# Attention of a two-layer hybrid block rebuilt: high and low values packed in one stationary tile, linear units inside the attention stages, first turns of a pair ahead of the next pair's scores

## What is computed

```python
def _gqa(q, k, v):
    s = jnp.einsum('bqkgd,bskd->bkgqs', q, k).astype(jnp.float32) * (HEAD_DIM ** -0.5)
    p = jax.nn.softmax(s, axis=-1).astype(v.dtype)
    return jnp.einsum('bkgqs,bskd->bqkgd', p, v)
...
        s = jnp.concatenate([s_nb.reshape(B, H, GRID_W, kr * kcn), s_ctx], axis=-1)
        p = jax.nn.softmax(s, axis=-1).astype(v.dtype)
...
def _merge(gz, oa, ob, oc, w_branch, w_out):
    ga, gb, gf = jnp.split(jax.nn.sigmoid(gz), N_BRANCH, axis=-1)
    y = ga * (oa @ w_branch[0]) + gb * (ob @ w_branch[1]) + gf * (oc @ w_branch[2])
    return y @ w_out
```

## Time and profile before

| | us |
|---|---|
| median of 3 runs (2630.68 to 2631.56) | 2631.35 |
| the profiled execution | 2630.05 |
| its span, first to last instruction | 2628.2 |
| TensorE busy | 2413.8 (92%) |
| VectorE busy | 1177.5 (45%) |
| ScalarE busy | 797.8 (30%) |
| GpSimd busy | 789.3 (30%) |
| mean granted clock of TensorE | 0.971 |

### The profile page before, as it was taken

One profiled execution on the slowest core, in us unless ns is written; L12 is line 12 of the kernel. 1 busy time (PEld: TensorE's weight loads), 2 busy tenths in 40 slices (PEclk: granted clock), 3 DMA queues, 4 the chain that ended last, 5 costly groups with the idle time before them and its releaser, 6 DMA issues. The chain is left out here.

```text
span 2628.2 us, 37990 instructions
## 1 busy us (share of the span) xinstructions
PE 2413.8 (92%) x13562; PEld 2184.1 (83%) x13562; DVE 1177.5 (45%) x2129; ACT 797.8 (30%) x1305; POOL 789.3 (30%) x368
## 2 busy tenths in 40 slices
PE   7989899998899949999999959999998996999996
PEld 2889889987799949999999948789887875788885
DVE  3784464132643175575572271646204543423234
ACT  4122353213532252211111142345224524322222
POOL 1322201332013232232232333320432044444444
PEclk9999999999999979999999979999999998999998
DMA  6621100141112332343342323110321134233333
GB/s 238 212 98 61 36 0 25 64 145 54 40 30 61 112 120 95 108 151 112 110 160 64 120 96 93 56 49 0 101 85 57 39 91 141 73 95 97 97 97 132
DMA packets 63019, 237.62 MB, mean 90 GB/s; under 512 B 7252, under 2 KB 7508, under 8 KB 61272
## 3 DMA queue, kind: packets, MB, share of 16 engines
q1 hardware_dynamic: 51552, 194.02, 22.8%
q10 hardware_dynamic: 11384, 42.48, 4.5%
HBM read 225.97 MB, written 10.49 MB: 90 GB/s over the span
## 5 line engine op out<-in xcount | busy, mean ns | idle before, releaser
L418 POOL TENSOR_TENSOR w_lo<-raw,w_hi 128x1024 fp32r<-128x1024 f32 x268 | 663.2, 2475 | 1460.1 <-ACT w_hi L525 1460.1
L525 ACT ACTIVATE w_hi<-raw 128x1024 fp32r<-128x1024 f32 x268 | 284.0, 1060 | 776.3 <-PE ps L1318 373.4
L1316 PE MATMUL ps<-h_hi,w_lo 128*128 128x384 f32 (+1 forms) x1152 | 419.3, 364 | 10.2 <-POOL h_lo L437 8.7
L1316 PE MATMUL ps<-h_hi,w_hi 128*128 128x384 f32 (+1 forms) x1152 | 416.6, 362 | 0.0
L1316 PE MATMUL ps<-h_lo,w_hi 128*128 128x384 f32 (+1 forms) x1152 | 416.6, 362 | 0.0
L1316 PEld LDWEIGHTS ps<-h_hi,w_lo 128*128 128x128 f32 x1152 | 216.3, 188 | 38.7 <-POOL h_lo L437 12.1
L1316 PEld LDWEIGHTS ps<-h_hi,w_hi 128*128 128x128 f32 x1152 | 216.2, 188 | 22.5
L1316 PEld LDWEIGHTS ps<-h_lo,w_hi 128*128 128x128 f32 x1152 | 216.3, 188 | 22.0
L1318 PE MATMUL ps<-h_hi,w_hi 128*128 128x384 f32 x576 | 192.4, 334 | 0.0
L1318 PE MATMUL ps<-h_lo,w_hi 128*128 128x384 f32 x576 | 192.4, 334 | 0.0
L1318 PE MATMUL ps<-h_hi,w_lo 128*128 128x384 f32 x576 | 192.4, 334 | 0.0
(11 more groups left out here) (175 smaller groups left out, 4522.6 us busy)
## 6 DMA issues: line engine op xcount, KB each, us to landing
raw<-in_stream SPq DMA_DIRECT2D x268, 512.0 KB, 3.6
ada_raw_gate_up<-in_w_ada SPq DMA_DIRECT2D x48, 512.0 KB, 6.0
ada_raw_fourier_in<-in_w_ada SPq DMA_DIRECT2D x24, 512.0 KB, 4.3
bias_sb<-in_bias ACTq DMA_DIRECT2D x16, 640.0 KB, 3.9
first_raw<-in_w_first SPq DMA_DIRECT2D x8, 1152.0 KB, 5.1
scratch<-xr ACTq DMA_DIRECT2D x16, 512.0 KB, 3.1
xr<-scratch ACTq DMA_DIRECT2D x14, 512.0 KB, 6.2
xr<-in_x_in ACTq DMA_DIRECT2D x8, 512.0 KB, 6.1
```

The source lines that it names most:

```text
L418: nc.gpsimd.tensor_tensor(w_lo[:, s, :], raw[:, s, :], w_hi[:, s, :].bitcast(F32), ALU.subtract).then_inc(S("lo_made"), 1)
L525: nc.scalar.activation(w_hi[:, s, :], raw[:, s, :], ACT.Copy).then_inc(S("hi_made"), 1)
L1316: last = nc.tensor.matmul(bank(0), tile, x[:, k, 0:split], start=start, stop=stop)
```

## The change

**Stages.** The gates of A (8 units) are computed inside attention A, and the later queries and keys of B (6 units) and the first two gates of B inside attention B. These are the fills: `fill` takes the 24 (or 48) steps of a unit and spreads them over the slots of a head. The merges of A and B shrink to 4 and 10 units, and `values`, with the first key unit, the first query unit and four value units, replaces `tokens_b`. Queries and keys of B come out of `columns` feature by feature, so they need no staging and no transposes; A's are transposed for two heads at once straight from `tok_a`. `stage` is gone from GpSimd.

**Attention.** The unit of work is a pair of query tiles, `ORDER` = (0,1), (3,2), (4,5); layer 1 has the first two. I call the handling of pair n a slot. Before the turns GpSimd multiplies `p_sb` with the reciprocal row sum (`normalise`). Turned blocks are split, `pt_hi` by ScalarE (`turned_hi`) and `pt_lo` by VectorE (`turned_lo`), in groups of at most 512 columns. The values are packed as [high | low] in one stationary tile of 128 columns, and each key tile takes two fp32r matmuls of up to 256 columns, one by `pt_lo` and one by `pt_hi`. The 128 output rows hold the high and the low share, which `move_half` (ScalarE) and `fold` (VectorE) add. `out_hi` (ScalarE) and `o_rest` (GpSimd) split the sum for the merge.

**Order.** In TensorE's program the first two groups of turns of pair n stand ahead of the scores of n+1. The attention loops are written out in full on all engines. The bias of B comes in two halves per head, the rope table is loaded in `tokens_a`, and several tiles have other places in SBUF.

```diff
+ORDER = ((0, 1), (3, 2), (4, 5))
...
-        add("merge", layer, t, 12, part=2)
-        add("attention", layer, t, part=0)
-        add("merge", layer, t, 12, part=0)
-        add("tokens_b", layer, t, 12)
-        add("attention", layer, t, part=1)
-        add("merge", layer, t, 12, part=1)
+        add("merge_c", layer, t, 12)
+        add("attention", layer, t, FILLS, part=0)
+        add("merge_a", layer, t, 4)
+        add("values", layer, t, 6)
+        add("attention", layer, t, FILLS, part=1)
+        add("merge_b", layer, t, 10)
...
+                def normalise(n, i):
+                    j, c = n % pairs, 2 * (n % 2) + i
+                    keys = P * len(key_tiles(branch, ORDER[j][i], i))
+                    pool.wait_ge(S("inverse"), at(ph, "inverse") + 2 * n + i + 1)
+                    p = p_sb[branch][n % 2][i][:, 0:keys]
+                    nc.gpsimd.tensor_tensor(p, p, row_inv[:, c:c + 1].broadcast_to([P, keys]), ALU.mult
+                                            ).then_inc(S("p_ready"), 1)
...
+                for n in range(HEADS * pairs):
+                    if n + 1 < HEADS * pairs:
+                        normalise(n + 1, 0)
+                    if n and (n - 1) // pairs % 2:
+                        o_rest(n - 1)
+                    if n + 1 < HEADS * pairs:
+                        normalise(n + 1, 1)
+                    f = fill_ended(ph, n - 1)
+                    if f is not None:
+                        lo_part(ph.unit + f + 2)
...
+                for n in range(count):
+                    groups = range(len(turn_groups(branch, n % pairs)))
+                    f = fill_ended(ph, n - 1)
+                    if n:
+                        move_half(n - 1)
+                    if f is not None:
+                        fill_out(f)
+                    turned_hi(n, 0)
+                    if n + 1 < count:
+                        probs(n + 1, 0)
+                    for g in groups[1:2]:
+                        turned_hi(n, g)
+                    if fill_halves(ph) == 2 and (n + 1) % pairs == 0 and n + 1 < count:
+                        gate_half((n + 1) // pairs, 0)
+                    if n and (n - 1) // pairs % 2:
+                        out_hi(n - 1)
+                    if n + 1 < count:
+                        probs(n + 1, 1)
+                    for g in groups[2:]:
+                        turned_hi(n, g)
+                    for name in slot_pieces(ph, n):
+                        piece(*name)
+                    if f is not None:
+                        act.wait_ge(S("unit_done"), ph.unit + f + 1)
+                        split(ph.unit + f + 2, f % 2)
+                        if branch == 1 and f < 6 and f % 2:
+                            key_copies(f // 2 + 1, at(ph, "fill_out") + f + 1)
+                    h, j = divmod(n, pairs)
+                    if branch == 1 and j < 2 and h + 1 < HEADS:
+                        load_bias(ph, h + 1, j)
+                move_half(count - 1)
+                out_hi(count - 1)
...
+                def turned_lo(n, g):
+                    order = turns["p", n, g]
+                    a, w = 512 * g, turn_width(branch, n % pairs, g)
+                    dve.wait_ge(S("hi_out"), at(ph, "hi_out") + order + 1)
+                    nc.vector.tensor_tensor(pt_lo[branch][:, a:a + w], ps[:, TURN_BANK[branch] + order % 2, 0:w], pt_hi[branch][:, a:a + w].bitcast(F32),
+                                            ALU.subtract).then_inc(S("lo_out"), 1)
...
+                def fold(n):
+                    h, j = divmod(n, pairs)
+                    a, rows = 2 * P * (n % 2), slice(HD * (h % 2), HD * (h % 2) + HD)
+                    dve.wait_ge(S("moved"), at(ph, "moved") + n + 1)
+                    if h > 1 and h % 2 == 0:
+                        dve.wait_ge(S("o_lo"), at(ph, "o_lo") + pairs * (h // 2 - 1) + j + 1)
+                    nc.vector.tensor_tensor(o_sum[branch][rows, j, :], ps[rows, OUT_BANK[branch], a:a + 2 * P], o_half[branch][rows, n % 2, :], ALU.add
+                                            ).then_inc(S("folded"), 1)
...
+                for n in range(count):
+                    groups = range(len(turn_groups(branch, n % pairs)))
+                    f = fill_ended(ph, n - 1)
+                    if n:
+                        fold(n - 1)
+                    if branch == 1 and f is not None and f < 6:
+                        filled = at(ph, "fill_out") + f + 1
+                        if f % 2:
+                            key_rest(f // 2 + 1, filled)
+                        else:
+                            query_rest(ph, f // 2 + 1, filled)
+                    if n + 1 < count:
+                        maximum(n + 1, 0)
+                        maximum(n + 1, 1)
+                    turned_lo(n, 0)
+                    if n + 1 < count:
+                        invert(n + 1, 0)
+                    for g in groups[1:2]:
+                        turned_lo(n, g)
+                    if n + 1 < count:
+                        invert(n + 1, 1)
+                    for g in groups[2:]:
+                        turned_lo(n, g)
+                    for name in slot_pieces(ph, n):
+                        piece(*name)
+                fold(count - 1)
...
+                                user = ORDER[j][0 if kt in key_tiles(branch, ORDER[j][0], 0) else 1]
+                                out_col, w = out_col + P * (user % 2), P
+                            a = 512 * g + 2 * P * x
+                            for pt in (pt_lo, pt_hi):
+                                last = nc.tensor.matmul(ps[:, OUT_BANK[branch], out_col:out_col + w], v, pt[branch][:, a:a + w],
+                                                        start=g == 0 and x == 0 and pt is pt_lo,
+                                                        stop=g == len(groups) - 1 and x == len(groups[g]) - 1 and pt is pt_hi,
+                                                        skip_group_check=True)
+                    if len(groups) - 1 in some:
+                        last.then_inc(S("attended"), 1)
...
+                for n in range(count):
+                    groups = range(len(turn_groups(branch, n % pairs)))
+                    for g in groups[:2]:
+                        turn(n, g)
+                    if n + 1 < count:
+                        score(n + 1, 0)
+                        score(n + 1, 1)
+                    fill(n, 0)
+                    for g in groups[2:]:
+                        turn(n, g)
+                    for name in slot_pieces(ph, n):
+                        piece(*name)
+                    attend(n, groups[:2])
+                    fill(n, 1)
+                    attend(n, groups[2:])
```

1116 lines of the change are left out of this document (633 added, 483 removed).

## The result

The changed kernel takes 2605.34 us (median of 4; 2595.60 to 2606.16), against 2631.01 for the kernel before in the same comparison: a ratio of 0.9894, with an interval of 0.9870 to 0.9917. Four more executions in a later comparison gave 2603.26 and 0.9898 (0.9882 to 0.9915). The forecast was 2605. It was right in size, but not every term behind it was, and one of the agreements is partly luck.

The account below looks back on a forecast made before the run. It saw TensorE's work and its pauses in the four attention stages as the bound. 635.8+13+9.6+7+398.4+17 = 1080.8 us against 1107.0, 26 less, gave 2605 us; forecast's own range 2570 to 2635, widened to 2565 and 2650.

Parts of the forecast that it names:

- The slot of A: Attention A: one query-tile pair with 768 keys takes 8.0 us, 8.7 where ScalarE also copies an output or gate.
- the 2% that I had added: Four attention stages: 13 us added, since the same walk gave 92.3 us for an old stage that takes 94.1.
- Normalising: GpSimd in attention: 1.42 us for 768 keys, priced by the add with a broadcast operand, 1.89 per 1024.
- the slow rival: GpSimd's in-place product takes 2.03 us for 768 keys and ends last; stages 43 us more, 2648 us; chance 0.15.
- The danger: VectorE held up while GpSimd works: said to be small here, as o_lo, which reads PSUM, stays under 0.70 us.
- The slot of B: Attention B: full slot 7.3 us, with the fill's bank emptied 8.4 or 9.0 to 9.4; 22.2 and 16.9 per head.
- the starts: Starts of the attention stages: 2.0 us twice for A, 2.8 us twice for B.
- the wait for the bias: Attention B of layer 1: half loads of the bias, taken as 3.2 us each, cost 7 us in all.
- 635.8 + 13 + 9.6 + 7: Four attention stages: walked lengths 635.8 us, plus the 2%, the stage starts and the bias wait.
- 398.4 + 17: Touched stages outside attention: 398.4 us, plus 17 for the fold ahead of merge B, values start and y_lo wait.
- The clock: Rival: with TensorE busy for some 76% of attention the granted clock could fall, 2635 to 2665 us; chance 0.05.
- 73 + 32: TensorE work saved: 73 us in probabilities times values, 32 us in transposes.

Follow-up runs that it names:

- Scores first: Changed kernel, but TensorE computes the scores of pair n+1 before the first two turns of pair n: 2548.01 us, ratio to before 0.9694.
- normalising: Changed kernel with GpSimd normalising only 16 of each tile's 256 to 768 keys, work left out: 2575.30 us, the four attention stages 19.0 us less.
- two thirds: Changed kernel with two thirds of each fill, in place of one half, ahead of the last turn: 2585.42 us.
- without half of the fills: Changed kernel with every second of the first 23 matmul steps of each half unit inside attention not issued: 2604.18 us.
- overlapped emptying: In branch B VectorE takes the first head's low part once ScalarE has copied that half: 2586.24 us on the changed kernel, 2536.31 with scores computed first.

## Why the prediction came true, step by step

**The slot of A.** Forecast 8.0 us for a full slot, 8.7 with a copied output or gate between the exponentials, 6.5 and 7.2 to 7.8 around the context pair. Measured 7.93, 8.60, 5.97 to 6.45, and 7.7 to 8.4. The walked lengths of the two stages, 188.0 and 140.6, were measured as 189.0 and 141.2 without the 2% that I had added. Scores first (forecast 50 less in the stages, measured 50.3), normalising (20, measured 19) and two thirds (A of layer 0: 183.7, measured 183.5) use the same terms, so the mechanism is shown and not only the sum.

**Normalising.** Forecast 1.42 us for 768 keys from the add with a broadcast operand in the earlier trace rows, measured 1.47. The in-place product of two full tiles, which the slow rival was built on, is not its like. In the earlier trace rows I read 0.96 to 2.68 us as the stretching of one instruction; they are two shapes, 128x768 at 0.96 in layer 0 and 128x512 at 2.68 in layer 1, where GpSimd works beside it. The danger is thus larger than I wrote for two tiles in SBUF, and the forecast does not rest on it: the new low parts, which read PSUM, took 0.68.

**The slot of B was mis-sized.** I had 22.2 us per head in layer 0; two heads in a row took 24.0 and 23.7 (blocks of scores begin at 590.95, 614.93 and 638.64), 3.3 more. One part is the emptying of the fill's bank, for which I had a slot of 8.4. The copies take 1.62 together and the low parts 1.92, TensorE's pause is 2.8 us, and at the key units, where a stretch at the lower clock follows, the slot lasts 9.6; at the query units it lasts 8.1 to 8.4. That is 0.9 of the 3.3. The larger part lies in the other slots. In every second head GpSimd also makes the low part of the output, 0.73 us between its two normalisings, and ScalarE the high one between the exponentials; there TensorE waits 0.89 us for p_sb in place of 0.20, and the two slots take 7.8 and 7.8 us against 7.0 and 7.4 in the head before. I had this copy in the slots of A and one figure for every head of B. In layer 1 it is the emptying: its slots take 10.1 to 10.5 and 9.5 us where I had 9.0 to 9.4. The B stages were walked as 307.2 and took 330.7. The two added percent, the starts and the wait for the bias covered most of that, for no reason of theirs: **the bias never made VectorE wait**, the half loads land in 2.9 us and no wait for a transfer stands in the B stage of layer 1. So 7 us were forecast for a wait that is not there.

**Stages and edges.** For the stages I had 635.8 + 13 + 9.6 + 7 = 665.4, of which 4 for the start of A lie in the merge of C by the stages' bounds above (it grew from 99.9 to 102.3 us in layer 0): 661.4 against 660.9 measured. The half microsecond is an agreement of errors, B too short and the additions too long. For the rest I had 398.4 + 17, measured 405.8. Edges were thus 7 us and not 17. The wait for y_lo, for example, is 1.9 us in the merge of B and project where the earlier trace rows had 2.4.

**The last 9 us are luck.** By the terms that the profile bears out, the forecast stood for the profiled execution at 1080.8 - 1107.0, 26 less, and that one is 34.4 shorter. The medians differ by 25.7: six of eight executions of the changed kernel ran at a clock of 0.962 to 0.965, and the kernel before at 0.968 to 0.973. The forecast held no such term; too much for edges stood in its place.

**The rivals.** Slow normalising is out (1.47 us). The clock did not fall in the stages as a whole, 0.96 to 0.99, but the rival was near: without half of the fills it holds. TensorE's share of busy time in the stages, forecast as 76%, is 82% in the profile's count, which counts matmuls until they end; my 494 us counted from start to start. The prices of matmuls held: values 0.119 us apart, transposes 0.109, fills of 384 columns 0.175.

**Where the expected gain went.** TensorE was given 73 + 32 = 105 us less to do, and 26 to 34 arrive. The scores-first run shows the larger part of the missing, 50 to 57 us: it is the time in which VectorE and GpSimd stand while TensorE turns pair n, before it makes the scores that they wait for. The overlapped emptying and the two thirds of a fill give another 24 us, after which the change is worth 107 us.
